# Attention stage: keys projected ahead of queries, softmax weights turned unscaled, most high halves made by ScalarE

## The reference, cut to what matters

```python
qkv = h @ w_qkv
q = head_rmsnorm(q, q_norm); k = head_rmsnorm(k, k_norm)        # per head, over its 64 channels
s = einsum('bqhd,bkhd->bhqk', qc, kb) * scale + bias            # per chunk of 64 queries
s = where(valid, s, -1e30)
p = softmax(s, axis=-1)
o = einsum('bhqk,bkhd->bqhd', p, vb)
return o @ w_o
```

## Time and profile before

| | us |
|---|---|
| median of 3 runs (lowest, highest) | 1697.71 (1696.97, 1697.93) |
| the profiled execution, its own time | 1696.46 |
| its span | 1694.7 |
| PE busy | 1617.2 (95% of the span) |
| DVE busy | 1245.4 (73%) |
| ACT busy | 751.8 (44%) |
| POOL busy | 473.2 (28%) |
| first matmul of block ATT+0 | at 222.01 |
| first matmul of block ATT+20 | at 304.26 |
| first matmul of block ATT+28 | at 339.48 |

### The profile page before, as it was taken

The page is one execution under the profiler, slowest core; times in us unless marked ns, Lnnn a source line. Parts: engine busy times, 40 slices in busy tenths (PEclk is TensorE's granted clock), DMA queues, the critical chain, the costliest instruction groups (busy, mean ns, idle before and its releaser), DMA issues.

```text
span 1694.7 us, 29073 instructions
## 1 busy us (share of the span) xinstructions
PE 1617.2 (95%) x11502; PEld 1487.2 (88%) x11502; DVE 1245.4 (73%) x2123; ACT 751.8 (44%) x1484; POOL 473.2 (28%) x308
## 2 busy tenths in 40 slices
PE   6999998999999899999898999999999999999999
PEld 6999976889999677889898999999999888888887
DVE  6666687576667676567789999999999655555555
ACT  6544534554455243111234444444444444444443
POOL 1111135211111432333267995333343000000000
PEclk9999999999999899999999999999999999999999
DMA  5556554355565544435434554445444465665654
GB/s 186 179 183 186 182 191 162 113 153 184 186 184 173 165 145 131 138 125 162 142 125 149 165 172 158 155 150 154 147 150 150 162 187 187 188 188 189 191 187 137
DMA packets 77478, 277.87 MB, mean 164 GB/s; under 512 B 8600, under 2 KB 9880, under 8 KB 77344
## 3 DMA queue, kind: packets, MB, share of 16 engines
q1 hardware_dynamic: 77344, 276.02, 51.6%
HBM read 274.94 MB, written 1.05 MB: 163 GB/s over the span
## 4 chain that ended last, share of the span: by engine, by line
PE 70%; DVE 22%; issue 4%; POOL 2%; ACT 2%; DMA 0%; DVEq 0%; SPq 0%; ACTq 0%; POOLq 0%
PE ps L828 70%; DVE WL L345 5%; DVE BIG L1281 4%; DVE XT L1281 2%; DVE OH L1281 1%; DVE HL L1284 1%; DVE BIG L1719 1%; POOL WH L405 1%; DVE SQN L1281 1%; DVE BIG L1714 1%; DVE BIG L1717 1%; DVE BIG L1712 1%; DVE BIG L1715 1%; DVE BIG L1751 1%; DVE BIG L1757 1%
## 5 line engine op out<-in xcount | busy, mean ns | idle before, releaser
L345 DVE TENSOR_TENSOR WL<-RAW,WH 128x1024 fp32r<-128x1024 f32 x455 | 565.9, 1244 | 223.5 <-ACT WH L473 158.3
L828 PE MATMUL ps<-HH,WH 128*128 128x256 f32 x2048 | 592.7, 289 | 17.4 <-DVE HL L1281 4.5
L828 PE MATMUL ps<-HL,WH 128*128 128x256 f32 x2048 | 581.3, 284 | 0.0
L828 PE MATMUL ps<-HH,WL 128*128 128x256 f32 x2048 | 580.8, 284 | 0.0
L473 ACT ACTIVATE WH<-RAW 128x1024 fp32r<-128x1024 f32 x329 | 345.7, 1052 | 204.4 <-PE ps L828 204.4
L828 PEld LDWEIGHTS ps<-HH,WH 128*128 128x128 f32 x2048 | 394.2, 192 | 23.5 <-issue 6.8
L828 PEld LDWEIGHTS ps<-HL,WH 128*128 128x128 f32 x2048 | 394.7, 193 | 1.0 <-issue 1.0
L828 PEld LDWEIGHTS ps<-HH,WL 128*128 128x128 f32 x2048 | 394.6, 193 | 0.0
L405 POOL CAST WH<-RAW 128x1024 fp32r<-128x1024 f32 x181 | 217.7, 1204 | 427.2 <-PE ps L828 424.3
L828 PE MATMUL ps<-WH,GH 128*128 128x512 f32 x512 | 203.0, 397 | 1.8 <-DVE GL L1281 1.8
L828 PE MATMUL ps<-WH,GL 128*128 128x512 f32 x512 | 202.9, 396 | 0.0
(11 more groups left out here) (229 smaller groups left out, 2369.2 us busy)
## 6 DMA issues: line engine op xcount, KB each, us to landing
RAW<-wall SPq DMA_DIRECT2D x510, 512.0 KB, 3.6
B<-rel SPq DMA_DIRECT2D x4, 768.0 KB, 5.5
DEC<-con SPq DMA_DIRECT2D x4, 384.0 KB, 4.2
XT<-xt SPq DMA_DIRECT2D x4, 256.0 KB, 5.3
out<-XT SPq DMA_DIRECT2D x4, 256.0 KB, 2.1
WIN<-con SPq DMA_DIRECT2D x1, 768.0 KB, 8.3
NMASK<-con SPq DMA_DIRECT2D x1, 192.0 KB
PAR<-par SPq DMA_DIRECT2D x1, 190.0 KB, 2.5
```

What stands on the lines that cost most here:

```text
L345: ins = eng.tensor_tensor(wl, RAW[:, b % NRAW, :], wh.bitcast(F), ALU.subtract)
L828: return pe.matmul(o, l, r, start=start, stop=stop, skip_group_check=True)
```

## The change

The groups are projected keys first (keys 0-7, queries 0-7, keys 8-15, queries 8-15), and the slots of squares, means, powers, roots, turning and taking are moved to fit. Keys are scaled by DVE right after their projection, and the next group for the same two banks (block ATT+8) waits for that. The scores are at other slots, and PE turns the exponentials unscaled, two slots after the scores. The values are computed with `PT` as the stationary operand and `VN` moving, so that the result has tokens on the partitions, in one bank for two pairs of heads; DVE multiplies it by the reciprocals into a new tile `AN` (`values_normed`), PE turns that (`values_turned`), and ACT and DVE make the halves of 128x512 at once. ACT makes the high halves of this stage but for ATT+1 and ATT+13, 15, 17, 19, 21, 23, 24 and 26, which stay on POOL; on POOL `group_power` now stands ahead of that slot's high half. Left out of the diff here: the new tile and the names of semaphores (`s_prob` goes, `s_an` and `s_at` come).

```diff
     ffn(0)
-    for g in (0, 2, 1, 3):
+    for g in (2, 0, 3, 1):
...
-ENTRY = [0, AT["gate0", 0], AT["qk", 0], AT["gate1", 0], AT["sqk", 0], AT["pq", 0]]
+ENTRY = [0, AT["gate0", 0], AT["qk", 8], AT["gate1", 0], AT["sqk", 0], AT["pq", 0]]
...
 SECOND = [b + 1 for b in ENTRY[1:]]
-ATT, MIX, PQ, UP, WP = AT["qk", 0], AT["sqk", 0], AT["pq", 0], AT["u", 0], AT["w", 0]
+ATT, MIX, PQ, UP, WP = AT["qk", 8], AT["sqk", 0], AT["pq", 0], AT["u", 0], AT["w", 0]
...
+HIGH_ATT = (13, 15, 17, 19, 21, 23, 24, 26)
 def high_on_pool(b):
-    return b in SECOND or ATT + 5 <= b < ENTRY[3] or MIX + 5 <= b < ENTRY[5] or UP + ROUTED + 4 <= b < WP
+    return b in SECOND or b - ATT in HIGH_ATT or MIX + 5 <= b < ENTRY[5] or UP + ROUTED + 4 <= b < WP
...
 NAT_LAST = [3, 7, 11, 15, 3, 7, 15, 19]
-NTR_BANK = [(0, 1), (2, 3), (4, 5), (6, 7), (0, 1), (2, 3), (6, 7), (4, 5)]
-SCALED = {1: 0, 3: 1, 4: 2, 5: 3}
+NTR_BANK = [(0, 1), (2, 3), (0, 1), (6, 7), (0, 1), (2, 3), (6, 7), (4, 5)]
+SCALED = {0: 0, 2: 1, 4: 2, 5: 3}
...
-SCO_SLOT = {12: 0, 13: 1, 15: 2, 16: 3, 19: 4, 20: 5, 22: 6, 23: 7}
-PV_SLOT = {20: (0, 1), 21: (2, 3), 24: (4, 5), 26: (6,), 27: (7,)}
+SCO_SLOT = {10: 0, 12: 1, 14: 2, 16: 3, 18: 4, 20: 5, 21: 6, 23: 7}
+PV_SLOT = {20: 0, 21: 1, 24: 2, 26: 3}
+VT_SLOT = {21: 0, 22: 1, 25: 2, 27: 3}
...
             for n in range(3, 30):
-                high(ATT + n + 2)
-                if n == 5:
+                if n in (5, 9, 13, 17):
+                    group_power(n // 4 - 1)
+                if n == 10:
                     power(2)
-                if n in (5, 8, 13, 16):
-                    group_power({5: 0, 8: 1, 13: 2, 16: 3}[n])
+                if high_on_pool(ATT + n + 2):
+                    high(ATT + n + 2)
...
                 for t_ in range(2):
-                    if g:
-                        act.wait_ge(s_nt, 2)
-                    act.activation(ANAT[:, 0, t_, :], bank[NAT_BANK[g][t_]][:, :], ACT.Copy).then_inc(s_nq, 1)
+                    if g == 3:
+                        act.wait_ge(s_nt, 4)
+                    act.activation(ANAT[:, 1, t_, :], bank[NAT_BANK[g][t_]][:, :], ACT.Copy).then_inc(s_nq, 1)
...
-            def weights(m):
-                act.wait_ge(s_rec, m + 1)
-                for i, (lo, hi) in enumerate(SPANS):
-                    for a in range(2):
-                        c, h = 4 * m + 2 * i + a, 2 * m + a
-                        act.activation(SS[:, h, lo:hi], SS[:, h, lo:hi], ACT.Copy, scale=RC[:, c:c + 1]).then_inc(s_prob, 1)
-            def values_high(m):
-                act.wait_ge(s_pv, 2 * (m // 2) + 2)
-                act.activation(AH[:, m, :], bank[PV_BANK[m // 2]][:, T * (m % 2):T * (m % 2) + T], ACT.Copy).then_inc(s_ah, 1)
+            def values_high(g):
+                act.wait_ge(s_at, g + 1)
+                act.activation(AH[:, 2 * g:2 * g + 2, :].rearrange("p k t -> p (k t)"), bank[PV_BANK[g]][:, :],
+                               ACT.Copy).then_inc(s_ah, 1)
...
             for n in range(3, 31):
-                if n in (4, 8, 12, 16):
-                    group_squares(n // 4 - 1, ASQ)
-                if n in (7, 12, 14, 19):
-                    g = {7: 0, 12: 1, 14: 2, 19: 3}[n]
-                    group_taken(g, (Q, K)[g % 2][:, 4 * (g // 2):4 * (g // 2) + 4, :], ("attn_q_norm", "attn_k_norm")[g % 2])
+                if n in (9, 10, 16, 18):
+                    g = {9: 0, 10: 1, 16: 2, 18: 3}[n]
+                    group_taken(g, (K, Q)[g % 2][:, 4 * (g // 2):4 * (g // 2) + 4, :], ("attn_k_norm", "attn_q_norm")[g % 2])
...
                     natural(VN, 1, (6, 7), ATT + 23)
-                if n - 4 in SCO_SLOT:
-                    weights_copied(SCO_SLOT[n - 4])
+                if n - 3 in SCO_SLOT:
+                    weights_copied(SCO_SLOT[n - 3])
+                if n in (8, 16):
+                    act.wait_ge(s_blk, ATT + NAT_LAST[n // 4 - 1] + 1)
+                    group_copied(n // 4 - 1)
+                if n in (4, 8, 12, 16):
+                    group_squares(n // 4 - 1, ASQ)
...
                     high(ATT + n + 2)
-                if n in (4, 12):
-                    group_copied(n // 4 - 1)
-                for m in PV_SLOT.get(n - 1, ()):
-                    values_high(m)
-                if n - 2 in SCO_SLOT:
-                    weights(SCO_SLOT[n - 2])
+                if n - 1 in VT_SLOT:
+                    values_high(VT_SLOT[n - 1])
...
                 else:
-                    pe.wait_ge(s_nq, g + 2)
+                    pe.wait_ge(s_nq, g + 1)
...
                     pe.wait_ge(s_ms, 3)
+                elif g == 2:
+                    pe.wait_ge(s_pt, 4)
...
             def turn(m):
-                pe.wait_ge(s_prob, 4 * m + 4)
-                if m:
+                pe.wait_ge(s_exp, 4 * m + 4)
+                if m == 2:
+                    pe.wait_ge(s_nev, 6)
+                elif m:
...
             def values(m):
-                o, c = bank[PV_BANK[m // 2]], T * (m % 2)
+                o = bank[PV_BANK[m // 2]]
...
                 for a in range(2):
-                    h, r = 2 * m + a, head_rows(a)
-                    mm(o[r, c:c + T], VN[:, 0, 64 * h:64 * h + 64], PT[:, h, 0:T], True, False)
-                    ins = mm(o[r, c + 128:c + T], VN[:, 1, 64 * h:64 * h + 64], PT[:, h, T:384], False, True)
+                    h, c = 2 * m + a, T * (m % 2) + 64 * a
+                    v0, v1 = (VN[:, t_, 64 * h:64 * h + 64] for t_ in range(2))
+                    mm(o[:, c:c + 64], PT[:, h, 0:128], v0, True, True)
+                    mm(o[:, c + 128:c + 192], PT[:, h, 128:T], v0, True, False)
+                    ins = mm(o[:, c + 128:c + 192], PT[:, h, T:384], v1, False, True)
                 ins.then_inc(s_pv, 1)
+            def values_turned(g):
+                pe.wait_ge(s_an, g + 1)
+                for i in range(4):
+                    ins = pe.transpose(bank[PV_BANK[g]][:, c128(i)], AN[:, g % 2, c128(i)], IDENT)
+                ins.then_inc(s_at, 1)
...
                 if k < 2:
-                    pe.wait_ge(s_al, 2 * k + 2)
+                    pe.wait_ge(s_al, k + 1)
...
                         pe.wait_ge(s_nsq, 2)
+                        pe.wait_ge(s_nsc, 2)
+                    elif n == 12:
+                        pe.wait_ge(s_nsq, 4)
                         pe.wait_ge(s_nq, 2)
-                    elif n == 12:
-                        pe.wait_ge(s_nsc, 2)
...
                 elif n < 24:
-                    if n % 4 == 0:
-                        pe.wait_ge(s_nev, 6 if n == 16 else 8)
+                    if n == 16:
+                        pe.wait_ge(s_nsc, 4)
+                    elif n == 20:
+                        pe.wait_ge(s_nev, 8)
...
                     m = n - 24
-                    pe.wait_ge(s_al, m + 1)
+                    pe.wait_ge(s_al, m // 2 + 1)
...
                 else:
-                    accumulate_last(b, [(AH[:, m, :], AL[:, m, :]) for m in (6, 7)], [(s_al, 7), (s_al, 8)], 4)
+                    accumulate_last(b, [(AH[:, m, :], AL[:, m, :]) for m in (6, 7)], [(s_al, 4), (s_al, 4)], 4)
...
                     norm_sum(2, bank[0])
-                if n in (6, 11, 13, 18):
-                    group_turned({6: 0, 11: 1, 13: 2, 18: 3}[n], ANAT)
-                if n - 3 in SCO_SLOT:
-                    turn(SCO_SLOT[n - 3])
+                if n in (8, 9, 15, 17):
+                    group_turned({8: 0, 9: 1, 15: 2, 17: 3}[n], ANAT)
...
                     scores(SCO_SLOT[n])
-                for m in PV_SLOT.get(n, ()):
-                    values(m)
+                if n - 2 in SCO_SLOT:
+                    turn(SCO_SLOT[n - 2])
+                if n in VT_SLOT:
+                    values_turned(VT_SLOT[n])
+                if n in PV_SLOT:
+                    values(2 * PV_SLOT[n])
+                    values(2 * PV_SLOT[n] + 1)
...
                     for t_, (lo, hi) in enumerate(SPANS):
-                        stt(SS[:, h, lo:hi], o[:, lo:hi], NR[0][:, 2 * (h // 8), t_, h % 8:h % 8 + 1], B[:, h, lo:hi], ALU.mult,
+                        stt(SS[:, h, lo:hi], o[:, lo:hi], NR[0][:, 2 * (h // 8) + 1, t_, h % 8:h % 8 + 1], B[:, h, lo:hi], ALU.mult,
...
-            def values_low(m):
-                dve.wait_ge(s_ah, 2 * (m // 2) + 2)
-                tt(AL[:, m, :], bank[PV_BANK[m // 2]][:, T * (m % 2):T * (m % 2) + T], AH[:, m, :].bitcast(F), ALU.subtract).then_inc(s_al, 1)
+            def values_normed(g):
+                dve.wait_ge(s_pv, 2 * g + 2)
+                dve.wait_ge(s_rec, 2 * g + 2)
+                if g >= 2:
+                    dve.wait_ge(s_at, g - 1)
+                tt(heads(AN[:, g % 2, :]), heads(bank[PV_BANK[g]][:, :]), RC[:, 8 * g:8 * g + 8].unsqueeze(2).to_broadcast(
+                    [128, 8, 64]), ALU.mult).then_inc(s_an, 1)
+            def values_low(g):
+                dve.wait_ge(s_ah, g + 1)
+                two = [x[:, 2 * g:2 * g + 2, :].rearrange("p k t -> p (k t)") for x in (AL, AH)]
```

(35 more changed lines are left out.)

## The result

The changed kernel takes 1703.33 us (median of 6 runs, 1702.72 to 1703.84) against 1697.47 for the kernel before: ratio 1.0036, 95% interval 1.0023 to 1.0049. That is 5.9 us slower; forecast were 8.7. The profiled execution has a span of 1702.0 us. I count the stage from the first matmul of b0 to the first of b28: 117.47 us before (222.01 to 339.48), 123.42 after (222.65 to 346.07), 5.95 more. Of these, 0.64 us lie before b20 and 5.31 from b20 to b28; forecast were 3.0 and 5.7. The rest of the program differs by the scatter of single executions.

The account below looks back on a forecast made before the run. PE, busy 95%, bounds the kernel, with waits and 1.2 GHz stretches in the attention stage. b20 3.0 later, values 3.7 and turning back 2.0 make +8.7 us: median 1706.4, own range 1703.5 to 1709 (chance 0.44), wider range 1697 to 1711.

Parts of the forecast that it names:

- b8 waits for scaling: Before b8, PE waits 1.9 us for DVE's scaling of keys 0-7, which ends at 246.25.
- Half a clock behind it: Behind b8's wait, 3.4 us of PE work at 1.2 GHz, 1.7 us lost.
- Biasing of pair 0 at 259.5, the third power at 271.2, b15 at 278.1 after 4.7 us of waiting: b15's cast on POOL stands behind the power of keys 8-15, so PE waits 4.7 us.
- b19 24.7 us behind b15, at 302.8: b19's cast likewise stands behind a power; PE needs 18 of the 24.7 us and waits 6 to 7.
- b20 3.0 us later: b20 starts at 307.3 against 304.26 before, including 1.7 us for one more stretch at 1.2 GHz.
- Values +3.7: Values with tokens on the partitions take 2.43 us a slot, +0.93 in each of four slots (3.0 to 5.2 in all).
- Turning back +2.0: 16 transposes of the values in four slots, with some 0.1 us for each start: +2.0 us of PE.
- No waits in the tail: PE doesn't wait in b20 to b31; normalizing and halves of the values are hidden behind blocks.
- A: Casts of b15 and b19 not late, third power started by 266.5: faster, -6.1 us, 1691.6; chance 0.14.
- Rival B: Waits form, but no lower clock behind those of b8 and b19: +5.3 us, 1703.0; chance 0.20.
- C: Only b15 waits, b19 starts at 296.1 and b20 at 298.9: +0.3 us, 1698.0; chance 0.12.
- D: Tail waits too, for the chain from values to halves of the last two groups: +4.6 us, 1711.0; chance 0.10.

Follow-up runs that it names:

- POOL's order: Changed kernel with POOL's high half ahead of that slot's power again (b15, b19), slots 13 and 17; ratio 1.0014 to the kernel before.
- slot 13 alone: Changed kernel with only slot 13 on POOL turned round (cast of b15 ahead of the power of keys 8-15); ratio 1.0033 to the kernel before.
- old values: Changed kernel with values in their old form, without softmax division and turning back, all slots kept; ratio 1.0013 to the kernel before.
- values twice: Every values matmul issued twice, in the changed kernel (1714.83 us) and in the kernel before (1702.6 us), one execution each.
- ACT's casts: ACT instead of POOL makes high halves: b15, b19 in the changed kernel, 1696.43 us; b8, b11, b16, b19 in the kernel before, ratio 0.9957.
- slot 7 mended too: Changed kernel with POOL's casts ahead of its powers and, in DVE's slot 7, root and scaling ahead of b9's low half; ratio 0.9983.
- slot 14: Changed kernel with POOL's casts ahead of powers, root and scaling ahead of the low half in DVE's slots 7 and 14; ratio 1.0005.

## Why the prediction was right

The sign, the mechanism and the places are right, and the size is 5.9 where 8.7 stood. The part behind b20 was sized well, 5.3 for 5.7; the part before it, 0.6 for 3.0, was not. By its own steps:

- *b8 waits for scaling:* 1.9 forecast, 1.83 measured, by the path given. *Half a clock behind it, 1.7:* not so in this execution, and b9 starts 1.6 us earlier for it than where the clock fell. Four of the experiments show the lower clock (POOL's order, slot 13 alone, old values, values twice: granted clock 0.72 over 246 to 252), the changed kernel and that with ACT's casts don't (1.00), all six with the same 1.83 us of idleness. The step took one row of 1.84 us for a rule.
- *Biasing of pair 0 at 259.5, the third power at 271.2, b15 at 278.1 after 4.7 us of waiting:* 259.73, 271.41, 277.41 after 4.59. That the first two agree within 0.3 is in part luck: the missing half clock is made up in the path by the root ahead of pair 0, put at 0.82 and measured at 1.63 (257.40 to 259.03) beside POOL's cast of b13, and by smaller amounts. Two experiments that take the cast from behind the power take the wait away.
- *b19 24.7 us behind b15, at 302.8:* 23.4, at 300.79. The mis-sized term is the path from the power to the block, put at 6.91 and measured at 6.0 both times (271.41 to 277.41, 294.79 to 300.79), since these powers took 2.90 us and not the 3.81 of the earlier trace rows.
- *b20 3.0 us later:* 0.64 later counted from b0 (82.89 against 82.25), 2.4 less than written. The two powers are 1.8 of it. The rest is the clock behind b8 (1.6), of which the root (0.8) and smaller steps give back 1.2, 0.3 that pair 2 was biased sooner behind b15, and 0.25 the other way from b19 to b20 (4.75 where 4.5 stood). Of the three stretches at 1.2 GHz two came.
- *Values +3.7:* 2.60 a slot against 1.50, +4.4, since a record costs 0.108 and not 0.101. The estimate from the Trainium skill, page "TensorE: Matmul & The Clock Gate", section "LDWEIGHTS (loading the stationary operand)", was 2.57 a slot and is the nearer one: the 2.60 measured and the loads in the timeline of PEld agree with it. *Turning back +2.0:* 0.49, 0.36, 0.36 and 0.35, 1.6. Together 6.0 against 5.7; b20 to b28 is 40.53 us against 35.22, +5.3. The changed kernel with the old values takes 34.77 there, so the other moves of the change gave some 0.5 back; no run says which.
- *No waits in the tail:* so it is.

Of the rivals, A (faster, 1691.6) is out, since the third power started at 271.41 and not by 266.5. It was too fast besides: with both casts in time the kernel is at 1.0014, and only with slot 7 mended too at 0.9983, about half of A's gain. Rival B is nearest in size, 5.3; half of it came true, as no half clock followed b8 in this execution, but the one behind b19 did come. C and D are out: b19 waited, the tail didn't. What ACT's casts and the order of keys first are each worth, no run takes apart.

## What to carry to other kernels

On an engine that takes its work in order, what stands in the queue behind a slow instruction inherits its inputs' lateness too: here a 1 us cast, whose low half the bound engine needed, stood behind a power that waited for another engine. Look for it by reading, for each wait of the bound engine, two releasers back; here that reading led to 11.7 us in the kernel before, with two edits (ACT's casts, root and scaling ahead of a low half). It is worth asking of such an edit whether the instruction moved ahead has its input yet: in slot 14 it hadn't, and the edit lost time. And turning a product round can cost more where it makes more and wider stationary loads, even if it moves fewer columns: 24 loads of 128 columns took 2.60 us, 16 of 64 took 1.50.

## What the runs showed of the hardware

- A power of 128x16 on POOL took 3.81 or 3.82 us in all 35 cases in which a low half had begun on DVE 0.16 to 0.17 us earlier (238.57 and 238.73 in the kernel after), and 2.90 in all 13 others (four powers in this stage in each of twelve executions). A low half that began 1.8 us into the power (252.64, the power of 250.82) left it at 2.90. For the third and the fourth power 2.90 became 3.81 when ACT made the casts. The cause isn't shown.
- 1.83 us of idleness of PE was followed by 1.2 GHz in four executions out of six with the same work up to there, and cost 1.6 us then. It was no different for longer waits: 2.78 us before b11 in the kernel before was followed by 1.2 GHz, 2.79 us before the same block in that kernel with the values twice was not; 2.65 to 2.68 us before the turning of keys 8-15 was in one of five executions (POOL's order). With waits of this size one profile doesn't tell what the clock will do.
- A float32 record with 128 stationary and 64 moving columns costs 0.108 to 0.112 us, one with 64 stationary and 128 or 256 moving 0.082 to 0.094.
